# Seven block products for both column halves of a down projection, with sums kept in device memory

## The reference, cut to what matters

```
n = rmsnorm(h, mlp_norm_w)                                    # h: 256 x 2048
h = h + square(relu(n @ w_up)) @ w_down                       # w_up: 2048 x 8192, w_down: 8192 x 2048
out = rmsnorm(h, final_norm_w)
```

## Time and profile before

| what | value |
|---|---|
| median of 3 runs | 1036.54 us (1036.47 to 1037.2) |
| profiled execution | 1036.7 us, its span 1034.9 us |
| mean granted TensorE clock | 0.998 |
| busy: TensorE matmul / VectorE / ScalarE / GpSimd | 1018.4 / 794.0 / 613.1 / 88.4 us |
| moved by DMA | 190.84 MB, mean 184 GB/s |

### The profile page before, as it was taken

The page is one execution under the profiler, slowest core; times in us unless marked ns, Lnnn a source line. Parts: engine busy times, 40 slices in busy tenths (PEclk is TensorE's granted clock), DMA queues, the critical chain, the costliest instruction groups (busy, mean ns, idle before and its releaser), DMA issues.

```text
span 1034.9 us, 14187 instructions
## 1 busy us (share of the span) xinstructions
PE 1018.4 (98%) x5547; PEld 881.3 (85%) x5547; DVE 794.0 (77%) x1086; ACT 613.1 (59%) x872; POOL 88.4 (9%) x151
## 2 busy tenths in 40 slices
PE   8999999999999998999999999999999999999997
PEld 7889999888887887888888888888888888888885
DVE  4655886988866479769968967976995996897594
ACT  4655855877764576546556645645664665564433
POOL 2134200732200000000000000000000000000002
PEclk9999999999999999999999999999999999999999
DMA  9576672243236546656666666666666666566553
GB/s 333 184 200 192 206 254 103 100 148 120 82 124 202 163 128 178 210 181 202 201 194 201 189 196 197 203 204 182 203 196 193 203 200 197 180 204 197 202 190 136
DMA packets 182798, 190.84 MB, mean 184 GB/s; under 512 B 9206, under 2 KB 145100, under 8 KB 182348
## 3 DMA queue, kind: packets, MB, share of 16 engines
q1 hardware_dynamic: 182300, 189.41, 58.2%
q10 hardware_dynamic: 432, 0.52, 0.1%
HBM read 187.82 MB, written 2.10 MB: 184 GB/s over the span
## 4 chain that ended last, share of the span: by engine, by line
PE 90%; DVE 6%; ACT 2%; issue 1%; DMA 0%; DVEq 0%; ACTq 0%
PE ps L2007 19%; PE ps L2075 12%; PE ps L2011 10%; PE ps L2082 6%; PE ps L1565 4%; PE ps L1566 4%; PE ps L2049 4%; PE ps L1569 4%; PE ps L2056 4%; PE ps L2050 4%; PE ps L1979 2%; PE ps L1856 2%; PE ps L1857 1%; PE ps L1860 1%; PE ps L1840 1%
## 5 line engine op out<-in xcount | busy, mean ns | idle before, releaser
L979 DVE TENSOR_TENSOR low<-raw,high 128x2048 fp32r<-128x2048 f32 x120 | 259.7, 2165 | 87.8 <-ACT high L826 86.9
L826 ACT ACTIVATE high<-raw 128x2048 fp32r<-128x2048 f32 x120 | 217.4, 1811 | 98.7 <-DMA raw<-in_w_up 75.7
L2007 PE MATMUL ps<-xT,high 128*128 128x512 f32 x896 | 212.9, 390 | 2.7 <-DVE hid L1377 2.7
L2007 PEld LDWEIGHTS ps<-xT,high 128*128 128x128 f32 x896 | 168.0, 188 | 39.1 <-DVE hid L1377 3.6
L979 DVE TENSOR_TENSOR w_lo<-raw,w_hi 128x1024 fp32r<-128x1024 f32 (+4 forms) x79 | 129.5, 1645 | 67.0 <-ACT w_hi L632 66.2
L632 ACT ACTIVATE w_hi<-raw 128x1024 fp32r<-128x1024 f32 (+3 forms) x75 | 104.1, 1391 | 64.6 <-PE ps L1569 40.9
L2075 PE MATMUL ps<-high,hidT 128*128 128x512 f32 x544 | 135.1, 390 | 0.0
L2011 PEld LDWEIGHTS ps<-xT,low 128*128 128x128 f32 x896 | 114.9, 191 | 4.4
L2075 PEld LDWEIGHTS ps<-high,hidT 128*128 128x128 f32 x544 | 100.4, 188 | 19.7
L2011 PE MATMUL ps<-xT,low 128*128 128x256 f32 x896 | 116.2, 283 | 0.0
L2082 PE MATMUL ps<-low,hidT 128*128 128x512 f32 x272 | 72.7, 389 | 0.0
(11 more groups left out here) (367 smaller groups left out, 1887.2 us busy)
## 6 DMA issues: line engine op xcount, KB each, us to landing
raw<-in_w_up SPq DMA_DIRECT2D x64, 1024.0 KB, 6.4
raw<-in_w_down SPq DMA_DIRECT2D x36, 1024.0 KB, 5.2
raw<-in_w_down SPq DMA_DIRECT2D x56, 512.0 KB, 4.7
raw<-in_w_o SPq DMA_DIRECT2D x16, 1024.0 KB, 5.2
raw<-in_w_in SPq DMA_DIRECT2D x8, 1024.0 KB, 5.3
raw<-in_w_in SPq DMA_DIRECT2D x8, 816.0 KB, 4.4
raw<-in_w_in SPq DMA_DIRECT2D x6, 832.0 KB, 8.6
raw<-in_mla_w_uq SPq DMA_DIRECT2D x12, 256.0 KB, 4.4
```

The costliest lines, as they stand in the source:

```text
L826: act.activation(high4[:, n % RAW, c0:2048], raw[:, n % RAW, c0:2048], ACT.Copy).then_inc(done, 1)
L979: return dve.tensor_tensor(dst, src, high.bitcast(F32), ALU.subtract)
L2007: pe.matmul(ps[:, 0, :].rearrange("p (c t) -> p c t", c=2), high4[:, s, P * k:P * k + P], xT[:, :, k, :], start=k == 0, stop=False)
```

## The change

All eight slots of groups 1 to 7 now use the seven products, in both column halves, with another set of sums of the same count (signs and pairs of weight and hidden sums differ; two hidden sums are made by one instruction of 256 columns). `down_half` stays for the last group alone. ScalarE now copies the seven banks to a stage in SBUF (`products_out`, twice a group: for half 0 ahead of its work of i = 4, for half 1 ahead of its work of i = 0 of the next group, the last after the loop). GpSimd then issues two DMAs (four banks and three) that write the stage to a tensor in device memory (group 1) or add it there (groups 2 to 7). VectorE's evictions are gone. After the loop SyncE loads the sums of each half back into SBUF ahead of the weight loads of blocks 4 to 7; VectorE merges half 0, splits the low half of block 4, merges half 1, splits block 5.

```diff
@@ SBUF
-        hid, acc, T_AT = seq(A_AT, ("hid", [P, 8, T], F32), ("acc", [P, TT, 1024], F32))
+        T_AT = A_AT + 3 * P
...
+        whole, e = seq(T_AT, ("whole", [P, 2, 7, 512], F32))
+        hid, acc, e = seq(T_AT + 4 * 4 * 2048, ("hid", [P, 8, T], F32), ("acc", [P, 1024], F32))
-        acc7, e = seq(Q_AT + 4 * TT * D, ("acc7", [P, 7, 512], F32))
+        stage, e = seq(Q_AT + 4 * TT * D, ("stage", [P, 7, 512], F32))
+        sums = nc.dram_tensor("product_sums", (P, 2, 7, 512), F32, kind="Internal").ap()
@@ SyncE
+            def load_quad(g, i):
+                n, half, k = down_at(g, i), i // 4, 2 * (i % 4)
+                place_free(n)
+                dst = raw[:, n % RAW, :].rearrange("p (b n) -> p b n", b=4)
+                for c, into in enumerate((dst[:, 1:3, :], dst[:, 0:4:3, :])):
+                    c0 = 1024 * half + 512 * c
+                    sp.dma_start(into, dn[:, g - 1, k:k + 2, c0:c0 + 512]).then_inc(raw_in[n % RAW], 16)
...
             for j in range(8):
+                if j == 4:
+                    for half in range(2):
+                        sp.wait_ge(stage_in, 32 * (2 * G - 3 + half))
+                        if half:
+                            sp.wait_ge(back, 16)
+                        sp.wait_ge(w_used, spent(down_at(G - 1, 7)))
+                        sp.dma_start(whole[:, half, :, :], sums[:, half, :, :]).then_inc(back, 16)
                 load_down(down_at(G, j), G - 1, 2 * (j % 4), j // 4)
@@ GpSimd
+            def add_products(g, half):
+                pool.wait_ge(prod_out, 7 * (2 * (g - 1) + half + 1))
+                for banks in (slice(0, 4), slice(4, 7)):
+                    if g == 1:
+                        pool.dma_start(sums[:, half, banks, :], stage[:, banks, :]).then_inc(stage_in, 16)
+                    else:
+                        pool.dma_start(sums[:, half, banks, :], stage[:, banks, :], accum_op=ALU.add).then_inc(stage_in, 16)
@@ ScalarE
+            def products_out(g, half):
+                m = 2 * (g - 1) + half
+                act.wait_ge(w_used, spent(down_at(g, 4 * half + 3)))
+                if m:
+                    act.wait_ge(stage_in, 32 * m)
+                for b in range(1, 8):
+                    act.activation(stage[:, b - 1, :], bank(b), ACT.Copy).then_inc(prod_out, 1)
...
                 for i in range(8):
+                    if i == 0 and g > 1:
+                        products_out(g - 1, 1)
+                    if i == 4:
+                        products_out(g, 0)
...
-                    if i < 3:
+                    if i < 7:
                         sums_hi(g, i + 1)
-                    elif i == 7 and g < G - 1:
+                    elif g < G - 1:
                         sums_hi(g + 1, 0)
...
+            products_out(G - 1, 1)
             down_weights_hi(G, 2)
@@ VectorE
-                    if i == 4:
-                        products_out(g, (4, 5, 6, 7))
...
-                    if i < 3:
+                    if i < 7:
                         weight_sums(g, i + 1)
                         down_weights_lo(g, i + 1)
                         weight_sums_lo(g, i + 1)
-                    elif i < 7:
-                        down_weights_lo(g, i + 1)
                     elif g < G - 1:
                         weight_sums(g + 1, 0)
-                        half_add(g)
                         down_weights_lo(g + 1, 0)
                         weight_sums_lo(g + 1, 0)
...
+            def merge(half):
+                dve.wait_ge(back, 16 * (half + 1))
+                for dst, x, y, op in (...seven combinations...):
+                    combine(half, dst, x, y, op)
+                for n, q in enumerate((1, 2, 3, 6)):
+                    ...
+                    dve.scalar_tensor_tensor(out=o, in0=whole[:, half, q, :], scalar=r1[:, t:t + 1], in1=o, op0=ALU.mult, op1=ALU.add)\
+                        .then_inc(merged, 1)
...
-            half_add(G - 1)
             hidden_parts(G - 1, 3)
-            down_weights_lo(G, 2)
...
+            for j in range(2, 4):
                 down_weights_lo(G, j)
-            dve.wait_ge(merged, 6)
+            merge(0)
+            down_weights_lo(G, 4)
+            merge(1)
+            down_weights_lo(G, 5)
+            dve.wait_ge(merged, 8)
             last_down()
@@ TensorE
                 for b in (1, 2, 3, 5, 7, 6, 4):
-                    if b == 1 and p == 0 and g > 1:
-                        pe.wait_ge(prod_out, 7 * (g - 1))
+                    if b == 1 and p == 0 and m:
+                        pe.wait_ge(prod_out, 7 * m)
...
             for g in range(1, G):
                 for i in range(8):
                     up_block(g, i)
-                    if i < 4:
-                        down_quad(g, i)
-                    else:
-                        down_half(g, i, 2048, i == 4, i == 7, half_t)
+                    down_quad(g, i)
```

More of the change, by code:

```diff
@@ L1354, in hidden_parts @@
                     a11, a12 = [hid[:, 2 * p + j, 0:P] for j in range(2)]
[L1355 to L1358, removed]
+                    near = hid[:, 2 * p:2 * p + 2, :].rearrange("p k (t n) -> p (k t) n", t=TT)[:, 0:4:3, :]
+                    s3, s1, s2, s4 = [s_sum[:, p, j, :] for j in range(4)]
+                    dve.tensor_tensor(s_sum[:, p, 0:2, :], hid[:, 2 * p:2 * p + 1, P:T].broadcast_to((P, 2, P)), near, ALU.subtract)\
+                        .then_inc(s_ok, 1)
                     dve.wait_ge(s_ok, q + 1)
-                    dve.tensor_tensor(s2, s3, a22, ALU.add).then_inc(s_ok, 1)
+                    dve.tensor_tensor(s2, s1, a11, ALU.subtract).then_inc(s_ok, 1)
                 hidden_lo(g, p)
@@ L1363, in hidden_parts @@
                     dve.wait_ge(s_ok, q + 2)
-                    dve.tensor_tensor(s4, a12, s2, ALU.subtract).then_inc(s_ok, 1)
+                    dve.tensor_tensor(s4, a12, s2, ALU.add).then_inc(s_ok, 1)
             def tile_sums_lo(g, p):
@@ L1478, in _, with combine @@
-            dve.wait_ge(half_out, 2 * (G - 1))
-            for t in range(TT):
-                merge(t, 1024, D, acc[:, t, :])
-            for j in range(4, 6):
-                down_weights_lo(G, j)
-            dve.wait_ge(merged, 6)
+            def combine(half, dst, x, y, op):
+                w = whole[:, half, :, :]
+                link(dve.tensor_tensor(w[:, dst, :], w[:, x, :], w[:, y, :], op))
+            def merge(half):
+                dve.wait_ge(back, 16 * (half + 1))
+                for dst, x, y, op in ((1, 0, 1, ALU.add), (0, 0, 5, ALU.add), (6, 6, 0, ALU.subtract), (0, 4, 0, ALU.subtract),
+                                      (2, 0, 2, ALU.add), (3, 3, 6, ALU.subtract), (6, 6, 4, ALU.add)):
+                    combine(half, dst, x, y, op)
+                for n, q in enumerate((1, 2, 3, 6)):
+                    t, c0 = n // 2, 1024 * half + 512 * (n % 2)
+                    o = h_sb[:, t, c0:c0 + 512]
+                    dve.scalar_tensor_tensor(out=o, in0=whole[:, half, q, :], scalar=r1[:, t:t + 1], in1=o, op0=ALU.mult, op1=ALU.add)\
+                        .then_inc(merged, 1)
@@ L2052, in down_quad, with down_half @@
                     if b == 1:
[L2053 removed]
+                        pe.wait_ge(dn_lo, s + 1)
                     if b == 5:
                         pe.wait_ge(sum_lo, s + 1)
[L2056 to L2061 removed]
+                    last = pe.matmul(bank(b), left[b](0), right[b](1), start=False, stop=p == 3)
+                last.then_inc(w_used, 1)
+            def down_half(i, base, start, stop):
+                g, n, p = G, down_at(G, i), i % 4
                 w = n % RAW
```

129 lines of the change are left out of this document (47 added, 82 removed).

## The result

The changed kernel takes 1107.97 us in the median of 4 runs (1106.56 to 1110.83), 1.069 times the kernel before (95% interval 1.068 to 1.071). The profiled execution took 1106.56 us, its span is 1104.7. The forecast was 1075, the range 1056 to 1112: the sign is right and the range holds it, but the time lies above the forecast's own case (1056 to 1100) and nearest to the rival "DMA is the wait" (1115).

The account below looks back on a forecast made before the run. TensorE bounds the kernel now; after the change VectorE would, at 88.7 us a group against 85.8. 1036.7 + 17 (loop) + 11 (DMA adds) + 10 (end) = 1074.7, say 1075 us; range 1056 to 1112.

Parts of the forecast that it names:

- the forecast's own case: Whole kernel: VectorE becomes the bound, with mild DMA contention, 1056 to 1100 us; chance 73%.
- DMA is the wait: Rival: adds at double price or worse delay every load near them, 17 + 45 + 16 = +78, 1115 us; chance 18%.
- PE's gain: Groups 1 to 7: all slots use seven products, 16.8 us less in all, 83.4 us a group on TensorE.
- VectorE's slot and hidden parts: Group loop: 9.11 us a slot, 72.9 a group, plus 7.8 for hidden parts and low halves: 80.7 us of work.
- The bubble: Slots 5 to 7: VectorE's up sum waits for ScalarE's up copy, 1.05 us three times, 3.2 us a group.
- The idle at the copies: VectorE waits behind ScalarE's seven product copies, 2.7 us at i = 4 and 2.1 at i = 0: 4.8 a group.
- The DMA adds: Fourteen 1.84 MB transfers beside the loads: 0.8 us each, +11 us; bounds from no cost to 45 us in all.
- The end: After the loop: last add, reload and merges delay the low halves TensorE needs, +10 us; +8 free, +16 at twice the price.
- No change: Rival: half of the idle, and the end's cost made up, time within 0.2% (2.1 us); chance 3%.
- PE stays the bound: Rival: without bubble or copy idle, VectorE's 80.7 us fit under TensorE's 83.4; 1020 to 1030 us; chance 6%.
- The signs: Profile after: 84 fewer matmuls, PE 93 to 95% busy, 89 to 91 us groups, 9.1 us VectorE slots, later up loads.
- Its third sign of being wrong: The prediction would be wrong if the loads' landing times dominate the waits; no size given.

Follow-up runs that it names:

- e1: The changed kernel with the adds of groups 2 to 7 cut to 64 columns of one bank: 1065.97 us, ratio 1.028.
- e10: e1 plus ScalarE copying 64 columns instead of seven banks in groups 2 to 7, and the up product before splitting tile sums: 1038.17 us, ratio 1.001.
- e9: e1 with ScalarE copying 64 columns of one bank instead of seven banks in groups 2 to 7: 1054.3 us, ratio 1.017.
- e2: The changed kernel with groups 2 to 7 overwriting the sums by plain writes of the same bytes instead of adding: 1096.37 us, ratio 1.059.
- e4: The changed kernel with each half's add issued as seven one-bank transfers spread over three slots, except the last half's, issued at once: 1077.82 us, ratio 1.040.
- e3: The changed kernel with ScalarE copying the up product out before it splits the tile sums: median 1101.68 us, four runs from 1095.73 to 1117.4.
- e13: e4 and e3 together, up split before copies, per-bank waits, and an end where VectorE adds the last products and splits low halves earlier: 1041.97 us, ratio 1.006.
- e5: e1 and e3 together: small adds, and the up product copied out before the tile sums are split: 1054.93 us, ratio 1.017.

## Why the prediction was right or wrong, point by point

The range was right by the part of it that it took from the rival "DMA is the wait": the forecast's own sum is 33 us short, and 29 of these are one step, the adds (42 us more than e1 where 11 + 2 were given to them).

- **PE's gain**, 83.4 us a group: right, and shown by e10 (82.5 to 83.6). In the kernel after nothing of it is left.
- **VectorE's slot and hidden parts**, 80.7 us of work a group: right, 80.97 us busy.
- **The bubble**, 1.05 us three times a group: right, 0.97. **The idle at the copies**, 2.7 and 2.1 us: 2.34 and 1.74, 0.7 less together; e9 shows that it is the copies'. With the adds cut the group is 88.6 for 88.7. That it fits to 0.1 is in part luck: e1's five waits come to 7.0 us of the 8.0 forecast, and 0.95 us of short gaps, which the sum didn't have, make it up (88.64 less 80.69 busy is 7.95). The loop is +20.8 for +17. By VectorE's up sums the first group costs 8.8, where one us was given to it, 4.7 of them the wait behind group 1's write; the last one, up to T, is 3.9 shorter than before.
- **The DMA adds**, 0.8 us a transfer, +11: the step that failed. The eleven adds that e1 cuts in the loop cost 31.7 us, 2.9 a transfer, between the two bounds but nearer to the upper one (45 for all); with the 4.7 of group 1's write it is 36. It failed twice. An add was priced as a plain transfer (3.3 us per MB; 4.6 measured), which is the part that the Trainium skill's rule had right, worth some 12 us (e2). And its effect was spread evenly in thought, "a slot's loads land in 6.4 and 5.3 us of 10.4, and only one or two meet each". In the trace a load beside a set of 1.84 MB takes up to 13.05 or 15.6 us, and by the prediction's own figures it has only some 5 us to spare in a slot (10.4 less 5.3). In a loop where VectorE has no slack, little of what is over is made up. e4 shows that most of it is the concentration: 30 us back with every byte still moved.
- **The end**, +10: 17.3 measured. Its chain in order of time, kernel after (T = 1035.96):
```profile
1040.33 15.14 DMA product_sums<-stage
1055.48 0.34 SPq L476
1055.87 10.09 DMA raw<-in_w_down
1065.99 1.92 ACT high L854
1067.93 2.29 DVE low L1020
...
1077.96 2.21 DVE low L1020
1080.21 1.21 PE ps L2099 x4
```
The path is the one forecast, station by station, but the last add is done at T + 19.5 and not T + 13, and all behind it moves by as much: block 4's low half at T + 34 for T + 28, block 5's at T + 44 for T + 38. Reload and load 4 together took 10.1 us for 11.3, the merge 7.7 for 7.7. The other us or so may be the clock, below. The bound "at twice the price +16" fits; e1's +8.6 fits the lower one.
- **No change** and **PE stays the bound**: refuted. e10 says what the latter would have needed: no copies, no bubble and no adds.
- **DMA is the wait**, 1115 and 18%: half right. Its sizes (45 in the loop, 16 in the end) are nearer to the measured 31.7 and 17.3 than mine. Its reason, the double price, is a quarter of the adds' cost.
- **The signs** that the prediction named say the same. 84 matmuls less, a busy share of 93%, VectorE's slot of 9.1 us and up loads that land later (6.7 us for 6.4) came true; a group of 89 to 91 us did not (93.1), nor did idle time only behind the copies and at the up sums. Its third sign of being wrong, loads that dominate the waits, holds in part: 84 us of waits for loads stand in the list above (62.6 on ScalarE, 21.4 on VectorE).

What stays open: why a plain write that lands in 9.3 us still costs about 30 us; group 1's first write in e1 shows only that an up load issued 0.6 us behind it landed 6.5 us later than the median one. That the write and the loads share the 16 engines is seen (DMA share 0.80 in the group above, 0.66 in e1's, 0.65 before), and DMA: Bandwidth & Descriptors (Issuing engines are not separate DMA queues) of the Trainium skill says the same; how the engines choose between the queues no run shows. Nor is it known why e3's runs scatter, or what the size of the transfers does in e4. Issuing loads earlier, once the low half is made, was not tried: the low half is written over the raw weights, so a place is not free before TensorE has used it.

## What to carry to other kernels

A background transfer is priced by the largest stretch of its bytes at once against the slack of one load, not by its mean share: twelve adds of 1.84 MB in two DMAs each cost 42 us, and the same bytes in pieces of 256 KB over three slots took 30 us less. When work leaves a busy engine by way of another engine and a DMA, write out that engine's order first: waits of 1 and of some 2 us at five places a group ate the whole gain on TensorE, and taking away one of them showed less than half of what both were worth.

## What the runs showed that was not expected

TensorE's granted clock can drop after short waits. Its timeline in the end, kernel after:
```profile
1055.86 1.98 PE L2092 MATMUL ps<-high,hidT 128*128 128x512 f32 x8
...
1068.00 3.69 PE L2092 MATMUL ps<-high,hidT 128*128 128x512 f32 x8 [9.25 <-issue]
...
1072.43 1.98 PE L2092 MATMUL ps<-high,hidT 128*128 128x512 f32 x8
```
and two stretches of it (columns as in the earlier trace rows, the granted clock third from the end):
```profile
1068.00:1071.50 3.50, 3.50 (x8) 2.79 (x9) 3.47 (x3) 2.23 (x2) 0.00 (x0) 0.50 1.02 410
1072.00:1077.00 5.00, 5.00 (x23) 3.92 (x21) 4.83 (x8) 3.02 (x2) 0.00 (x0) 1.00 0.55 220
```
The same eight matmuls take 1.98 us before a wait of 9.25 us, 3.69 us behind it at a clock of 0.50 (1.2 GHz), and 1.98 again 4.4 us later. In e13 a wait of 1.99 us was enough:
```profile
979.99 3.59 PE L2102 MATMUL ps<-high,hidT 128*128 128x512 f32 x8 [1.99 <-ACT stage L895]
```
So a wait on TensorE can cost 1.6 or 1.7 us more than it lasts. It need not: in e5 a wait of 1.98 us (before 567.47) was followed by 3.5 us at a clock of 1.00, one of 2.01 us (before 653.81) by 3.2 us at 0.69. The mean clock is 0.974 after and 0.998 before; that is why TensorE's busy time grew (1025.6 for 1018.4 us) with fewer matmuls. Where the waits come from late loads, this can be part of what they cost: from 395 us to T TensorE is busy for 590.8 us in the kernel after and for 574.4 in e1, with the same matmuls, 16.4 us more. How much of that reaches the 31.7 us isn't known; VectorE waits no longer for the up copy in the one than in the other (17.4 us, 18 times, in both).
